# Eight instead of six blocks of gate products beside the index scores, and the gate third of the modulation moved to the branch stage

## What is computed

```python
shift, scale, gate = jnp.split(jax.nn.silu(c) @ ada_w + ada_b, 3, axis=-1)
h = rmsnorm(x, g_pre) * (1 + scale[:, None]) + shift[:, None]
z = h @ w_in
a_conv, g_conv, q, k, v, g_attn, qi, ki, wi, gm = split_in(z)
y_c, conv_new = conv_branch(a_conv, conv_prev, conv_w, conv_b, ln_g, ln_b)
y_c = (y_c * jax.nn.silu(g_conv)) @ w_conv_out
o = sparse_attention(q, k, v, qi, ki, wi, past, rel_bias)   # index scores -> top 256 keys -> softmax
y_a = (o * jax.nn.silu(g_attn)) @ w_attn_out
gm_c, gm_a = jnp.split(jax.nn.sigmoid(gm), 2, axis=-1)
y = rmsnorm((gm_c * y_c + gm_a * y_a) @ w_out, g_post)
return x + gate[:, None] * y
```

## Time and profile before

| | |
|---|---|
| time, median of 3 runs | 3591.16 us (3586.13 to 3596.66) |
| the profiled execution | 3593.3 us, its span 3591.6 us |
| PE busy | 3432.5 us, 96% of the span |
| DVE busy | 2725.5 us, 76% |
| ACT, POOL busy | 1436.8 us and 1142.8 us |
| index scores, first to last matmul | 333.7 to 585.4 us |
| gate stage's last product ends | 1834.9 us |
| attention's first score matmul, branch's first product | 1853.6 us, 2970.0 us |

### The profile page before, as it was taken

The page is one execution under the profiler, slowest core; times in us unless marked ns, Lnnn a source line. Parts: engine busy times, 40 slices in busy tenths (PEclk is TensorE's granted clock), DMA queues, the critical chain, the costliest instruction groups (busy, mean ns, idle before and its releaser), DMA issues. The chain is left out here.

```text
span 3591.6 us, 50100 instructions
## 1 busy us (share of the span) xinstructions
PE 3432.5 (96%) x19221; PEld 2956.8 (82%) x19311; DVE 2725.5 (76%) x4130; ACT 1436.8 (40%) x1779; POOL 1142.8 (32%) x897
## 2 busy tenths in 40 slices
PE   6989999999999899999989999999999999989998
PEld 3989888999999899999976666666666669989987
DVE  2522788999899979999968888887887765676443
ACT  2312567889800000010025555555555550234121
POOL 2222112543334000000024644634643324665200
PEclk9999999999999999999989999999999999999999
DMA  7375537455555633544443113113111106667443
GB/s 254 114 245 167 149 119 168 164 170 178 182 182 182 236 123 141 185 158 163 154 121 69 33 31 74 33 31 71 33 31 35 33 27 223 201 213 258 138 143 117
DMA packets 389540, 480.25 MB, mean 134 GB/s; under 512 B 49249, under 2 KB 315633, under 8 KB 387830
## 3 DMA queue, kind: packets, MB, share of 16 engines
q1 hardware_dynamic: 331141, 283.29, 26.9%
q10 hardware_dynamic: 48112, 157.27, 12.5%
q0 software_dynamic: 10112, 37.49, 2.6%
HBM read 296.97 MB, written 187.02 MB: 135 GB/s over the span
## 5 line engine op out<-in xcount | busy, mean ns | idle before, releaser
L1126 PE MATMUL psum<-ha,gt 128*128 128x352 f32 x8136 | 1352.3, 324 | 11.2 <-DVE gq_lo L1344 7.3
L1126 PEld LDWEIGHTS psum<-ha,gt 128*128 128x128 f32 x8136 | 1323.0, 189 | 14.8 <-issue 8.7
L1414 DVE SCALAR_TENSOR_TENSOR cv<-cv,vecs,cv 128x1056 f32<-128x1056 f32 (+1 forms) x480 | 598.9, 1331 | 0.0
L2021 DVE TENSOR_TENSOR at_plo<-at,at 128x1024 fp32r<-128x1024 f32 (+2 forms) x308 | 437.3, 1420 | 147.9 <-ACT at L1924 146.0
L1923 ACT ACTIVATE at<-psum 128x1024 f32<-128x1024 f32 (+2 forms) x308 | 293.1, 952 | 439.5 <-PE psum L1796 389.8
L1846 PE MATMUL psum<-at,at 128*128 128x512 f32 (+5 forms) x688 | 334.8, 496 | 20.2 <-POOL at L1731 10.0
L707 PE MATMUL psum<-br,br 128*128 128x352 f32 x2016 | 338.2, 328 | 14.5 <-DVE br L2394 10.4
L707 PEld LDWEIGHTS psum<-br,br 128*128 128x128 f32 x2016 | 331.0, 191 | 19.3 <-issue 11.7
L1749 POOL TENSOR_TENSOR at<-at,cv 128x256 f32<-128x256 f32 (+2 forms) x272 | 223.4, 824 | 366.8 <-DVE at L1976 362.8
L781 DVE TENSOR_SCALAR_CACHE_REDUCE gl<-gt,gl 128x1792 bf16<-128x1792 f32 (+8 forms) x263 | 337.7, 1350 | 1.2
L1257 ACT ACTIVATE gt<-psum 128x1056 f32<-128x1056 f32 x80 | 84.0, 1050 | 613.3 <-PE psum L1126 592.1
(11 more groups left out here) (271 smaller groups left out, 4864.3 us busy)
## 6 DMA issues: line engine op xcount, KB each, us to landing
scratch_ws<-gt SPq DMA_DIRECT2D x112, 512.0 KB, 4.0
gt<-scratch_ws ACTq DMA_DIRECT2D x110, 512.0 KB, 4.9
gt<-in_w_in_dram SPq DMA_DIRECT2D x60, 512.0 KB, 5.8
scratch_gm<-gt ACTq DMA_DIRECT2D x32, 528.0 KB, 3.0
br<-scratch_gm ACTq DMA_DIRECT2D x32, 528.0 KB, 3.8
scratch_m<-br POOLq DMA_DIRECT2D x32, 528.0 KB, 5.7
at<-scratch_q SPq DMA_DIRECT2D x128, 128.0 KB, 2.9
scratch_u<-gl POOLq DMA_DIRECT2D x16, 528.0 KB, 3.7
```

What stands on the lines that cost most here:

```text
L1126: return nc.tensor.matmul(of[:, j, 0:W // 3], part[:, c, :], a[:, c, j * (W // 3):(j + 1) * (W // 3)], start=(c == 0 and k == 0), stop=(c ...
L1414: ins = nc.vector.scalar_tensor_tensor(to[:, 0:width], mine[:, k_:k_ + width], tap, to[:, 0:width], ALU.mult, ALU.add)
L2021: nc.vector.tensor_tensor(plo[j % 3][:, 0:len(mine), 0:n], prob[j % 3][:, 0:len(mine), 0:n], phi[j % 3][:, 0:len(mine), 0:n].bitcast(F32), ...
```

## The change

1. `FRONT` goes from 6 to 8. Of the 576 fills, 36 (`AHEAD`) are issued ahead of the first piece, where the 36 idle products stood; the other 540 are spread to the last piece (before: 432, spread so that they ended ahead of the last tile). In both halves four pairs of `gm` instead of three stand ahead of `u`.
2. The gate third leaves the gate stage. Its weights (4 MB) are loaded in one DMA in the attention stage after the store of unit 53, over buffers that are no longer used (for which the key buffers change places), and its 64 matmuls run at the beginning of the branch stage, in place of the idle products there.
3. The idle products at the attention stage's beginning are gone.

```diff
-        QI, FRONT, E = 8, 6, 2
+        QI, FRONT, E = 8, 8, 2
...
-        FILL = FRONT * PER
+        FILL, AHEAD = FRONT * PER, PER // 2
...
-            have = fill_after[-1] if fill_after else 0
-            want = min(FILL, seen * (FILL + PER // 2) // sum(sizes))
+            have = fill_after[-1] if fill_after else AHEAD
+            want = AHEAD + seen * (FILL - AHEAD) // sum(sizes)
...
                 queries(k)
-                if k % 2 == 0 and k // 2 - 1 < GATED:
-                    gate_weights(k // 2 - 1)
...
-            idle_products(nc, mem.bank(0), mem.ident, 36)
             count = done = 0
+            while done < AHEAD:
+                beside(done)
+                done += 1
             for k, (t, g) in enumerate(units):
-                if k % 2 == 1 and 0 <= k // 2 - 1 < GATED:
-                    gate_columns(k // 2 - 1)
...
+            def gate_third():
+
+                sp.wait_ge(s_acc, 3 * NTL)
+                sp.dma_start(gate_w[:], w["ada_w"][0].rearrange("(c p) n -> p c n", p=P)[:, :, 2 * D:3 * D]).then_inc(mem.s_third, 16)
...
                     store(u)
+                    if u == 3 * NTL + 2:
+                        gate_third()
...
-                if h == 0 and c == 0 and u < 2:
-                    idle_products(nc, acc, mem.ident, 20)
...
                         pe.wait_ge(s_fhi, 1)
-                        idle_products(nc, acc, mem.ident, 12)
...
-            idle_products(nc, mem.bank(7), mem.ident, 24)
-            pe.wait_ge(pr.s_hi, 1)
-            idle_products(nc, mem.bank(7), mem.ident, 8)
+            pe.wait_ge(mem.s_third, 16)
+            for f in range(KC):
+                for c in range(KC):
+                    last = nc.tensor.matmul(modt[:, 2 * f:2 * f + 2], gate_w[:, c, f * P:(f + 1) * P], mem.mod[:, 2, c, :], start=(c == 0), stop=(c == KC - 1))
+            last.then_inc(s_gmm, 1)
```

More of the change, by code:

```diff
@@ L123, in __init__ @@
         self.s_last = nc.alloc_semaphore(name="last_merged")
+        self.s_third = nc.alloc_semaphore(name="gate_third")
         self.base = (nc.sbuf_base + 63) // 64 * 64
@@ L127, in __init__, with gate_third_at @@
         self.end = self.base + size - 64
+    def gate_third_at(self):
+        return self.base + 2 * ((4 * KC * W + 63) // 64 * 64)
     def bank(self, n):
@@ L1513, in pair, with attention_stage @@
         return s if 0 <= s < len(self.pairs) else None
-def attention_stage(nc, mem, x, out, scr, masks):
+def attention_stage(nc, mem, x, w, out, scr, masks):
     total = score_offset(NT) + SKEYS
@@ L1546, in attention_stage @@
                            + [([P, 2, GROUP, 4], F32), ([P, 2, GROUP], F32)])
[L1547 removed]
+        masks_, kst, k2, vst, vraw = parts[0], [parts[3], parts[1]], [parts[4], parts[2]], parts[5:7], parts[7]
         bias, bth, btl = parts[8:10], parts[10:12], parts[12:14]
@@ L1569, in attention_stage @@
         FRONT = KPAD // 2
+        gate_w = nc.alloc_sbuf_tensor_at("at_gate_w", [P, KC, D], F32, offset=mem.gate_third_at())
+        assert mem.at["at3"] <= mem.gate_third_at() and mem.gate_third_at() + 4 * KC * D <= mem.at["at6"]
         ktmp0 = nc.alloc_sbuf_tensor_at("at_ktmp0", [P, KPAD], F32R, offset=mem.at["at22"])
@@ L2026, in _, with branch_stage @@
                     columns(u)
-def branch_stage(nc, mem, x, w, out, scr):
+    return gate_w
+def branch_stage(nc, mem, x, w, out, scr, gate_w):
     runs = [(half, name) for name in ("a", "c") for half in range(2)]
@@ L2041, in branch_stage @@
                            + [([P, W], F32)] * 6 + [([P, 2, D], F32)] + [([P, KC, P], F32R)] * 2 + [([P, D], F32)])
+        assert mem.at["br2"] == mem.gate_third_at() and mem.gate_third_at() + 4 * KC * D <= mem.at["br3"]
         acts = [parts[0:2], parts[2:4]]
@@ L2067, in branch_stage @@
         s_third = sem("third")
+        s_gmm, s_gmod = sem("gmm"), sem("gmod")
+        modt = mem.bank(7)[:, 0:2 * KC]
         gains = [mem.psum[k % 2][:, 1536:2048] for k in range(4)]
@@ L2258, in spread @@
             def spread(k):
+                pe.wait_ge(s_gmod, 2)
                 if k >= 2:
@@ L2271, in turn @@
                 pe.wait_ge(s_tail, 32)
+                pe.wait_ge(s_gmod, 1)
                 if k:
@@ L2404, in _ @@
                                         ALU.subtract).then_inc(s_flo, 1)
+            dve.wait_ge(s_gmm, 1)
+            nc.vector.tensor_tensor(mem.mod[:, 2], modt.rearrange("p (c s) -> p c s", c=KC),
+                                    mem.vecs[:, :, R_ADAB + 2:R_ADAB + 3].to_broadcast([P, KC, 2]), ALU.add).then_inc(s_gmod, 1)
+            dve.wait_ge(s_gmod, 1)
+            nc.vector.tensor_tensor(mem.gate_g[:], mem.mod[:, 2],
+                                    mem.vecs[:, :, R_GPOST:R_GPOST + 1].to_broadcast([P, KC, 2]), ALU.mult).then_inc(s_gmod, 1)
             for n, (r, k, b) in enumerate(BLOCKS):
@@ L2570, in build @@
         if upto >= 6:
-            attention_stage(nc, mem, x, out, scr, masks)
+            gate_w = attention_stage(nc, mem, x, w, out, scr, masks)
         if upto >= 7:
-            ready = branch_stage(nc, mem, x, w, out, scr)
+            ready = branch_stage(nc, mem, x, w, out, scr, gate_w)
         if upto >= 8:
```

16 lines of the change are left out of this document (removed).

## The result

The changed kernel takes 3607.02 us (median of 20 runs, 3593.95 to 3615.82) against 3590.78 us before (20 runs): ratio 1.0047, 95% interval 1.0038 to 1.0057. It is slower by 16 us, outside the range of 3578 to 3603. The profiled execution has a span of 3604.5 us, 12.9 us more than before.

What follows compares the result with a forecast made beforehand. PE was read as 96% busy, with DVE's path 7.8 us behind it at the gate stage's end. Gate stage -4, attention +1 +1, branch +2 sum to 0 against the profiled 3593.3 (median 3591.2): 3591 us, range 3578 to 3603.

Steps and rivals of the forecast that it cites:

- the branch stage's +2: Branch stage's beginning: gate third takes 17.8 us, first product held by its data anyway; +2 us, between 0 and +6.
- Index scores, -3: Index scores: gate third gone -15.3, fills +17.6, last tile's hidden fills -5.4, clock -2, pauses and split +2; sum -3 us.
- 12.2 + 8 + 2: Scores and gate stage: 12.2 us of fills outside the last tile, 8 us wait at block 11, 2 us slow work behind it.
- The load behind the bias copies, 8 us: Gate stage: block 11's load queues behind the bias copies, its split ends at 615.3, PE needs it at 607.1; waits 8 us.
- The tie of DVE's end to the `u` blocks: Gate stage: DVE's end hangs on when PE makes the second half's `u` blocks, so two fewer blocks bring it no earlier.
- the sum was +4: DVE's path to the gate stage's end: -3 scores, +8 wait, +2 slow restart, -3 into the second half; +4 us.
- the -3 of the prediction: Into the gate stage's second half: two kinds of load no longer meet at PE's restart; -3 us, between 0 and -7.
- The margin of 7.8 us: Gate stage's end before the change: DVE's path is only 7.8 us behind PE's, and this is subtracted from DVE's shift.
- Attention stage: Attention stage: removing idle products gains nothing, low clock costs +1 us, query loads late behind the 4 MB load +1 us.
- (a): Rival, gate stage: no stall at block 11; 3581 us, or 3576 with scores at -5 and a quieter restart; chance 0.15.
- (b): Rival, gate stage: PE's two blocks are gained whole because DVE's end is not tied; 3569 us, chance 0.04.
- (c): Rival: slower, PE waits 14 us + 2 at block 11, late query loads +6, branch start +4; 3606 us, chance 0.13.

Runs made afterwards that it cites:

- run 6: The changed kernel with 64 idle products of 128 columns straight ahead of the gate third, no wait between: 3624.3 us, ratio 1.0100 to the kernel before.
- run 8: The changed kernel with the gate third computed with the weights moving, 512 columns at a time: 3594.3 us, ratio 0.9999 to the kernel before.
- run 2: The kernel before with only the gate third moved to the branch stage, six blocks kept: 3591.8 us, ratio 1.0008.
- run 11: The kernel before with only the gate third moved to the branch stage and computed there with the weights moving: 3576.7 us, ratio 0.9976.
- run 4: The changed kernel with three pairs of `gm` instead of four ahead of `u` in the second half: 3589.2 us, ratio 0.9999 to the kernel before.
- run 5: The changed kernel with an identity product of 128 columns behind each matmul of the gate third: 3636.0 us, ratio 1.0121 to the kernel before.
- run 10: The changed kernel with three `gm` pairs ahead of `u` in the second half and the gate third's weights moving: 3576.7 us, ratio 0.9964 to the kernel before.

## Why the prediction was wrong, step by step

**The step that failed is the branch stage's +2.** The prediction put it as: "The gate third is 128 instructions busy for 14.8 us (...) and begins as slowly: 14.8 + 3 = 17.8". It took the duration from a place where dense score matmuls surround each eight of them, and the clock's rise from identity products. Measured were 27.44 us. From the stage's first PE instruction to the end of the first two products it takes 53.2 us, against 2982.55 + 14.84 - 2958.83 = 38.6 in the earlier trace rows: +14.6. The step's own sum with the right size gives it: +2 as predicted, 27.4 - 17.8 = 9.6 for the gate third, and half of the 5.2 us for which the window of 2980 to 2990 shows the clock at half (0.74), 2.6: 14.2. That the clock was the cause is shown by runs 6 and 8. Of the stage's other 1.7 us, 0.9 lie in the pause of PE ahead of the output stage (3.32 us instead of 2.46); the rest I didn't follow.

The prediction weighed the rule of the Trainium skill (TensorE: Matmul & The Clock Gate, What's actually happening) only for the attention stage. By the Trainium skill there, the default is the throttled clock and activity releases it. In the branch stage the trace shows PE 100% busy for 27.4 us and no release, so busy time in the record is not by itself the activity meant.

**Index scores, -3:** +3 in the profile, and by chance on either side. The changed kernel and the nine others that keep its fills took 249.8 to 256.5 us, 253.1 in the mean, against 252.7. By parts, the gate third was worth 13.1 (252.7 less the mean of runs 2 and 11, 239.0 and 240.2) instead of 15.3, and the two blocks cost 253.1 - 239.6 = 13.5 instead of 12.2. In the last tile the clock rose to 1.00, as predicted; that all 33 fills there were hidden was not tested by itself. One sign of being wrong, scores that end later than 587, came in this profile (587.9), though DVE did not set their pace: its sums still have 35.8 us of idle time ahead of them.

**What two blocks are worth to PE.** Behind the scores PE is spared 2 blocks, 23.4 us. Nothing is left of it: 13.5 us more in the scores, 8.35 of stall and 1.6 of slow work behind it (28 records in 6.18 us instead of 4.6) are 23.5. The prediction's own terms, 12.2 + 8 + 2, come to 22.2, but it never set them beside the 23.4. Counted from the gate stage's first product, PE ends after 1599.6 us in the changed kernel and after 1597.9 and 1600.6 in runs 2 and 11 with six blocks.

**The load behind the bias copies, 8 us:** right. 8.35 us at block 11. The split ended at 620.1 and not at 615.3, and PE came to block 11 at 611.8 and not at 607.1. Both hang on the end of the scores, since the copies are issued behind the last unit's queries, so this is no luck: from the copies' issue to the split's end it took 46.6 us instead of 50.0, -3.4 where -4 was taken for the emptier queue.

**The tie of DVE's end to the `u` blocks:** right, and shown by run 4. Where the sum was +4, the first gated product shows +7.1 (1276.7 to 1283.8), as does DVE's end; the difference is about that of the index scores, which ended 1.5 us later and not 3 sooner. The restart's wait went from 6.43 to 3.55 us, the -3 of the prediction. The wait of the first gated product was to grow to about 30 us and is 23.6. The margin of 7.8 us was then just used up, so the gate stage gave 0.7 us instead of 4. PE idles for 31.5 us; 20 to 30 were named.

**Attention stage:** right in that neither the idle products nor the 4 MB load show. From the stage's start to the first score matmul of the stream (L1784, L1771) it takes 36.0 us instead of 35.8. The +2 in the sum was not there: the stage is 5.3 us shorter, within the spread of all kernels.

**Rivals.** (a) is refuted by the stall and (b) by DVE's end. (c) gave 3606 us and 3607.0 was measured, but by a mechanism that it doesn't name: the stall had the size of the forecast, not of the rival, and the branch start cost 16 us instead of 4. The range left out the one unknown that mattered, since the gate third's cost at the new place had no upper bound of its own: all at half clock is 128 x 0.21 = 27 us, by the 29 records in 6.17 us that the kernel before itself needs from 2958 to 2965, in the slow beginning of the earlier trace rows.

## What to carry to other kernels

A matmul's duration holds only for its surroundings. When matmuls of few columns are moved from between dense work to a place of their own, cost them at half clock as the upper end, and look whether the long operand can be the moving one. And when work is taken off the busiest engine, find what the second engine's end is tied to: with a fourth pair ahead of the `u` blocks, DVE took back all that the gate third had freed on PE, and putting the order back gave 18.8 us. Last, work moved beside other work has a price there: the two blocks cost as much in the scores and in the stall as they saved behind them, and what they gain in the better order was too small to measure.

## What the runs showed of the hardware

- 64 float32 matmuls of 2 columns, back to back with their weight loads: the granted clock stays at half for 27.4 us with PE and PEld 100% busy, and falls some 4 us into them where it had been full (run 6). With 128-column identity products between them it stayed at half for 54 us (run 5). With 512 columns moving it rose after about 3 us in run 8, and after 5 to 6 us in runs 10 and 11 (0.50 in the window of the first 4 us, 0.92 and 0.96 in the rest). Such a record takes 0.42 us at full clock (run 8) and 0.8 us at half (run 10, 5 in 4.00 us).
- A two-column matmul costs no less than one of 128 columns: 0.214 us for a record at half clock, as much as the mean of the two kinds in run 5 (54.6 us for 256 records), and 0.108 at full (run 6). PEld is busy as long as PE in all of these windows; that the weight load sets the price is argued from that and was not tested.
- The first weights of the branch stage land later in every kernel with eight blocks beside the scores. POOL's first split starts 10.4 us behind the stage's start in the changed kernel and 10.6 to 12.0 us in the nine others of its kind, but 5.9 us in the kernel before and 6.1 and 5.8 us in runs 2 and 11, which have six, and which also keep the idle products of the attention stage. In run 8 it then holds PE up by 2.03 us. POOL's first split in the kernel before, and then in run 8:

```profile
2964.68 1.89 POOL L675 TENSOR_TENSOR br<-br,ones 128x1024 fp32r<-128x1024 f32 x1 [3.49 <-DMA br<-in_w_attn_out_dram]
```

```profile
2969.23 1.94 POOL L680 TENSOR_TENSOR br<-br,ones 128x1024 fp32r<-128x1024 f32 x1 [9.56 <-DMA br<-in_w_attn_out_dram]
```

The transfers issued there are the same, but SP takes 5.01 us to issue its part of `scratch_a` in the changed kernel (5.1 to 6.7 in the nine others) and 1.41 us before and in run 2. Why was not tested and stays open.
